# Latent attention's key rows copied in two groups of four, ScalarE copies of two output projections' banks, and a last stage that ends in token rows

## The reference, cut to what matters

```python
def sandwich(x, fn, pre_g, post_g, shift, scale, gate, res_w):
    hn = rmsnorm(x, pre_g) * (1 + scale[:, None, :]) + shift[:, None, :]
    y = rmsnorm(fn(hn), post_g)
    return x + res_w * gate[:, None, :] * y

def mla(h, w_in, q_norm, w_q_up, kv_norm, w_kv_up, w_o):
    ...
    k_rope = jnp.broadcast_to(rope(k_rope, pos), (B, S, MLA_HEADS, QK_ROPE))
    k = jnp.concatenate([kv[..., :QK_NOPE], k_rope.astype(kv.dtype)], axis=-1)
    ...
    return o.reshape(B, S, MLA_HEADS * V_HEAD) @ w_o

for i in range(2):
    # three sandwiches: ffn, mixer (latent attention for i = 0, dilated attention for i = 1), ffn
    x = sandwich(x, ffn_first, ...)
    x = sandwich(x, mixer, ...)
    x = sandwich(x, ffn_second, ...)
```

## Time and profile before

| | us |
|---|---|
| median of 3 runs | 4057.21 |
| lowest, highest | 4056.83, 4060.22 |
| the profiled execution's own time | 4056.78 |
| its span in the trace | 4055.0 |
| TensorE busy in the span | 3844.4 |
| VectorE busy | 2327.4 |
| ScalarE busy | 1291.5 |
| mean granted TensorE clock, share of full | 0.967 |

### The profile page before, as it was taken

The page is one execution under the profiler, slowest core; times in us unless marked ns, Lnnn a source line. Parts: engine busy times, 40 slices in busy tenths (PEclk is TensorE's granted clock), DMA queues, the critical chain, the costliest instruction groups (busy, mean ns, idle before and its releaser), DMA issues.

```text
span 4055.0 us, 48035 instructions
## 1 busy us (share of the span) xinstructions
PE 3844.4 (95%) x19230; PEld 3121.4 (77%) x19230; DVE 2327.4 (57%) x3024; ACT 1291.5 (32%) x1689; POOL 824.1 (20%) x580
## 2 busy tenths in 40 slices
PE   7998999999899999998899999999999999989997
PEld 6676888777688878886677888788777877767886
DVE  5876555587655555575566545543744554565333
ACT  4453232345323232224542222222233323322212
POOL 2100544210054436542222620000000000000000
PEclk9998999999899999998999999999999999999999
DMA  5111544311154435542223543233222112112331
GB/s 154 56 42 55 151 140 140 99 58 47 47 152 140 140 109 156 143 130 58 58 61 90 156 117 96 73 104 94 73 84 71 55 60 81 58 52 70 98 103 52
DMA packets 556442, 377.73 MB, mean 93 GB/s; under 512 B 30122, under 2 KB 553867, under 8 KB 556219
## 3 DMA queue, kind: packets, MB, share of 16 engines
q1 hardware_dynamic: 555642, 372.55, 31.3%
q10 hardware_dynamic: 576, 2.10, 0.1%
HBM read 372.44 MB, written 2.17 MB: 92 GB/s over the span
## 4 chain that ended last, share of the span: by engine, by line
PE 80%; DVE 15%; ACT 3%; issue 2%; DMA 0%; DVEq 0%; ACTq 0%; SPq 0%
PE bank L441 60%; PE bank L477 5%; PE bank L449 3%; DVE w_lo L419 2%; PE bank L822 2%; PE bank L807 2%; PE bank L2006 1%; PE bank L2031 1%; DVE conv_sum L1146 1%; PE bank L2052 1%; DVE hgrn_scores L1315 1%; PE bank L815 1%; ACT w_hi L410 1%; DVE norm_tmp L1531 1%; DVE std L849 1%
## 5 line engine op out<-in xcount | busy, mean ns | idle before, releaser
L441 PE MATMUL bank<-H_hi,w_hi 128*128 128x512 f32 x2384 | 996.5, 418 | 0.1
L441 PE MATMUL bank<-H_hi,w_lo 128*128 128x512 f32 x2384 | 933.2, 391 | 0.0
L441 PE MATMUL bank<-H_lo,w_hi 128*128 128x512 f32 x2384 | 931.8, 391 | 0.0
L419 DVE TENSOR_TENSOR w_lo<-w_raw,w_hi 128x2048 fp32r<-128x2048 f32 (+3 forms) x285 | 735.6, 2581 | 261.7 <-ACT w_hi L410 251.9
L410 ACT ACTIVATE w_hi<-w_raw 128x2048 fp32r<-128x2048 f32 (+3 forms) x285 | 529.2, 1857 | 300.4 <-DMA w_raw<-in_ffn_w_up 132.2
L441 PE MATMUL bank<-U_hi,w_hi 128*128 128x512 f32 x1408 | 558.4, 397 | 16.1 <-DVE U_lo L1195 10.3
L441 PE MATMUL bank<-U_hi,w_lo 128*128 128x512 f32 x1408 | 551.7, 392 | 0.0
L441 PE MATMUL bank<-U_lo,w_hi 128*128 128x512 f32 x1408 | 551.1, 391 | 0.0
L441 PEld LDWEIGHTS bank<-H_hi,w_hi 128*128 128x128 f32 x2384 | 449.0, 188 | 122.1 <-issue 39.2
L441 PEld LDWEIGHTS bank<-H_lo,w_hi 128*128 128x128 f32 x2384 | 449.6, 189 | 101.5 <-issue 21.0
L441 PEld LDWEIGHTS bank<-H_hi,w_lo 128*128 128x128 f32 x2384 | 448.1, 188 | 98.0 <-issue 0.3
(11 more groups left out here) (344 smaller groups left out, 4905.4 us busy)
## 6 DMA issues: line engine op xcount, KB each, us to landing
w_mod_raw<-in_w_mod SPq DMA_DIRECT2D x144, 512.0 KB, 6.4
w_raw<-in_ffn_w_gate SPq DMA_DIRECT2D x88, 512.0 KB, 4.0
w_raw<-in_ffn_w_up SPq DMA_DIRECT2D x88, 512.0 KB, 5.3
w_raw<-in_dil_w_in SPq DMA_DIRECT2D x36, 1024.0 KB, 5.1
w_raw<-in_w_mlp_in SPq DMA_DIRECT2D x32, 1024.0 KB, 5.5
w_raw<-in_w_mlp_out SPq DMA_DIRECT2D x32, 1024.0 KB, 5.2
w_raw<-in_ffn_w_down SPq DMA_DIRECT2D x32, 1024.0 KB, 5.1
w_raw<-in_w_in SPq DMA_DIRECT2D x16, 1024.0 KB, 5.2
```

The lines of the kernel that those rows point to most:

```text
L419: dve.eng.tensor_tensor(WL[u % SLOTS][:, 0:n], RAW[u % SLOTS][:, 0:n], WH[u % SLOTS][:, 0:n].bitcast(F32), ALU.subtract).then_inc(lo_done. ...
L441: mm = pe.eng.matmul(bank[0:m, :], w[:, k, c0:c0 + m], r[:, k, :], start=(k == 0 and i == 0), stop=(k == kt - 1 and i == 2))
```

## The change

It has three parts.

1. In latent attention ScalarE's eight copies of the rotated key rows become two groups of four. The first (slots of heads 0 to 3) stands in part 0 between the second and the third evacuation of `mla_kv`; the other (heads 4 to 7) in part 1 at point 9. TensorE's scores wait for four copies at their first head and for four more at the fifth.
2. In `mla_out` and `dil_out` ScalarE copies each bank to `Y` (`out_act`), and VectorE (`out_dve`) is left with products and sums; it waits for the bank to be freed.
3. The last stage turns while it multiplies. TensorE weaves in four transposes of `X` after the third inner tile of tile t, and four of `Y` times its gate (made by VectorE in `XY`) after the sixth inner tile of tile t+1; ScalarE copies both to token rows (`XROW`, `YROW`). When the sums are known, VectorE does one pass of 1024 for each block of 128 tokens, `XROW + YROW * rstd`, and SyncE's queue stores each block. The spread of factors, the sixteen passes over `X`, `sync_all`, the epilogue's transposes and its copies are gone.

The diff, cut to its core (the unchanged parts and the removed epilogue are left out):

```diff
+        def turn_x(pe, t):
+            pe.eng.wait_ge(x_rows.sem, t)
+            for b in range(NB):
+                mm = pe.eng.transpose(banks[6][:, b * P:(b + 1) * P], X[:, t, b * P:(b + 1) * P], EYE)
+            mm.then_inc(x_turned.sem, x_turned.add())
+        def turn_y(pe, t):
+            pe.eng.wait_ge(y_gated.sem, t + 1)
+            pe.eng.wait_ge(y_rows.sem, t)
+            ...
+        def last_down_pe(pe):
+            at_point = {}
+            for t in range(DT):
+                at_point[8 * t + 2] = (turn_x, t)
+                at_point[8 * t + 13] = (turn_y, t)
...
+            for u in lin[("ffn_down", 1, 1, 2)]:
+                pe_unit(pe, u, weave)
+            pe_running_sums(pe)
+            turn_y(pe, DT - 1)
...
+                    row_copy(act, x_turned, banks[6], XROW, x_rows, t)
+                    if t:
+                        row_copy(act, y_turned, banks[7], YROW, y_rows, t - 1)
+                    place, turn = acc_place[units[u]["tiles_at"] + j]
+                    act.eng.wait_ge(acc_free[place].sem, turn)
+                    ...
+                    act.eng.activation(SQ[t % 2][:], Y[:, t, :], ACT.Square)...
+            act_std(act, D, True)
+            row_copy(act, y_turned, banks[7], YROW, y_rows, DT - 1)
...
+                    ve.tensor_tensor(Y[:, t, :], Y[:, t, :], bank[:], ALU.add)...
+                    if t >= 2:
+                        dve.eng.wait_ge(y_turned.sem, t - 1)
+                    ve.tensor_scalar(XY[t % 2][:], Y[:, t, :], AFF[:, 1, 1, t:t + 1], None, ALU.mult)...
...
+            for b in range(NB):
+                ve.scalar_tensor_tensor(XROW[:, b, :], YROW[:, b, :], RSTD[:, b:b + 1], XROW[:, b, :], ALU.mult, ALU.add)...
+        def store_rows(sp):
+            for b in range(NB):
+                sp.eng.wait_ge(out_rows.sem, b + 1)
+                sp.eng.dma_start(io["out"][0, b * P:(b + 1) * P, :], XROW[:, b, :])...
...
+        def out_act(act, stage, dil=1):
+            ...
+                    bank, free = acc_take(act, u, j)
+                    act.eng.activation(in_order(Y[:, t, :], dil), dilated(bank[:], dil), ACT.Copy)...
+                    if t >= 2:
+                        act.eng.wait_ge(sq_summed.sem, sq_summed.next(act, 0 if t == 3 else 1))
+                    act.eng.activation(SQ[t % 2][:], Y[:, t, :], ACT.Square)...
+        def out_dve(dve, stage, two):
+            ...
+                    dve.eng.wait_ge(acc_free[place].sem, turn)
+                    x_product(dve, t, two)
+                    if 1 <= t < DT - 1:
+                        add_squares(dve, t, two)
+                        add_products(dve, t)
+            split_lo(dve, lin[stage][-1] + AHEAD)
...
-                    if i == 0:
-                        pe.eng.wait_ge(key_rows.sem, key_rows.next(pe, 8))
+                    if i < 24:
+                        pe.eng.wait_ge(key_rows.sem, key_rows.next(pe, 4))
...
+            def rope_rows(part):
+                if part == 0:
+                    act.eng.wait_ge(mla_rows.sem, mla_rows.next(act))
+                for h in range(4):
+                    ae.activation(MK[NOPE:QK, mla_slot(4 * part + h), :], MK0[NOPE:QK, :], ACT.Copy)...
...
+                    if (part, p) in ((0, 13), (1, 9)):
+                        rope_rows(part)
```

More of the change, by code:

```diff
@@ new lines, in build @@
+        x_turned, x_rows, y_gated, y_turned, y_rows, out_rows, out_stored = (line(n) for n in (
+            "x_rows_turned", "x_rows_ready", "y_gated_ready", "y_rows_turned", "y_rows_ready", "out_rows_ready", "out_stored"))
+        def turn_x(pe, t):
[7 more added lines that the diff above has]
+            for b in range(NB):
+                mm = pe.eng.transpose(banks[7][:, b * P:(b + 1) * P], XY[t % 2][:, b * P:(b + 1) * P], EYE)
+            mm.then_inc(y_turned.sem, y_turned.add())
@@ new lines, in last_down_pe, with weave @@
+        def last_down_pe(pe):
[3 more added lines that the diff above has]
+                at_point[8 * t + 13] = (turn_y, t)
+            points = iter(range(8 * DT))
+            def weave():
+                turn, t = at_point.get(next(points), (None, 0))
+                if turn:
+                    turn(pe, t)
+            for u in lin[("ffn_down", 1, 1, 2)]:
+                pe_unit(pe, u, weave)
+            pe_running_sums(pe)
+            turn_y(pe, DT - 1)
@@ new lines, in last_down_dve @@
+        def last_down_dve(dve):
+            stage, ve = ("ffn_down", 1, 1, 2), dve.eng
+            for u in lin[stage]:
+                if u != lin[stage][-1]:
+                    split_lo(dve, u + AHEAD)
+                for j in range(2):
+                    t = 2 * (u - lin[stage][0]) + j
+                    if t >= 2:
+                        add_squares(dve, t - 1)
+                    bank, free = acc_take(dve, u, j)
+                    ve.tensor_tensor(Y[:, t, :], Y[:, t, :], bank[:], ALU.add).then_inc(free.sem, free.add())
+                    dve.eng.wait_ge(free.sem, free.made)
+                    if t >= 2:
+                        dve.eng.wait_ge(y_turned.sem, t - 1)
+                    ve.tensor_scalar(XY[t % 2][:], Y[:, t, :], AFF[:, 1, 1, t:t + 1], None, ALU.mult).then_inc(y_gated.sem, y_gated.add())
+                    dve.eng.wait_ge(y_gated.sem, y_gated.made)
+            dve.eng.wait_ge(std_ready.sem, std_ready.next(dve))
+            ve.reciprocal(RSTD[:, 0:NB], STD[:, 0:NB]).then_inc(dve.step.sem, dve.step.add())
+            dve.eng.wait_ge(dve.step.sem, dve.step.made)
+            dve.eng.wait_ge(x_rows.sem, DT)
+            dve.eng.wait_ge(y_rows.sem, DT)
+            for b in range(NB):
+                ve.scalar_tensor_tensor(XROW[:, b, :], YROW[:, b, :], RSTD[:, b:b + 1], XROW[:, b, :], ALU.mult, ALU.add).then_inc(out_rows.sem, out_rows.add())
+                dve.eng.wait_ge(out_rows.sem, out_rows.made)
@@ L1571, in build @@
+        def store_rows(sp):
+            for b in range(NB):
+                sp.eng.wait_ge(out_rows.sem, b + 1)
+                sp.eng.dma_start(io["out"][0, b * P:(b + 1) * P, :], XROW[:, b, :]).then_inc(out_stored.sem, out_stored.add(16))
+            sp.eng.wait_ge(out_stored.sem, out_stored.made)
         SG = [at(f"silu_gate{i}", e_at + 2 * K * i, [P, L]) for i in range(2)]
@@ L1831, in mla_act @@
                             att_act_step(act, items, mla_bufs, kind, i)
-                if part == 0:
-                    act.eng.wait_ge(mla_rows.sem, mla_rows.next(act))
-                    for h in range(8):
-                        ae.activation(MK[NOPE:QK, h, :], MK0[NOPE:QK, :], ACT.Copy).then_inc(key_rows.sem, key_rows.add())
-                        act.eng.wait_ge(key_rows.sem, key_rows.made)
-            act_linear(act, ("mla_out",), running_squares(("mla_out",), y_tile), later=True, early=lin[("mla_out",)][:-1])
+            out_act(act, ("mla_out",))
         mla_rows = line("mla_key_rope_rows")
@@ L1890, in mla_dve @@
             sandwich_next(dve, 0, 1)
-            dve_linear(dve, ("mla_out",), to_y(("mla_out",), False, two=1), later=True, early=lin[("mla_out",)][:-1])
+            out_dve(dve, ("mla_out",), 1)
         CHUNKS = 3 * NB
@@ L2243, in dil_dve @@
             sandwich_next(dve, 1, 1)
-            dve_linear(dve, ("dil_out",), to_y(("dil_out",), False, dil=NB, two=0), later=True, early=lin[("dil_out",)][:-1])
+            out_dve(dve, ("dil_out",), 0)
         def second_pe(pe):
@@ L2493, in _ @@
                     dil_sp(sp, c)
+            store_rows(sp)
         @block.gpsimd
```

93 lines of the change are left out of this document (53 added, 40 removed).

## The result

| | before | changed |
|---|---|---|
| median, run side by side (4 runs each) | 4058.72 us | 4030.32 us |
| lowest to highest | 4056.83 to 4060.82 | 4029.13 to 4031.78 |
| span of the profiled execution | 4055.0 | 4028.2 |

The ratio is 0.993, with a 95% interval from 0.9913 to 0.9947, that is 22 to 35 us less. The forecast was 29.3 us less, at 4027.9; measured are 28.4 less, at 4030.32. Of the 2.4 us between forecast and median 1.5 lie in the kernel before, whose median was 1.5 us higher this time.

The account below looks back on a forecast made before the run. TensorE, busy 3844.4 of 4055.0 us, was taken as the bound, other engines costing time only where it waits. Gains of 3.1 + 6.7 + 8.1 + 11.4 = 29.3 us off 4057.2 gave 4027.9, range 4020 to 4037.

Parts of the forecast that it names:

- Key rows: Latent attention's first scores: start 3.4 us earlier, less 0.3 for the second four copies; 3.1 us gained, from 0.8 to 4.8.
- mla_out's border: Sums behind mla_out start earlier and run faster, less GpSimd's interference: 6.7 us gained, from 4.3 to 9.2.
- I take the middle, 4.4: Start of mla_out's border sums: 4.4 us earlier, between 3.7 (two copies beside GpSimd save nothing) and 5.1.
- The clock: mla_out's border: three to four of five groups of sums at the high clock, 3.0 us gained, from 2.0 to 4.1.
- GpSimd in the border: mla_out's border: GpSimd's next vector meets the first passes, a loss of 0.7 us, from 0 to 1.4.
- dil_out's border: Behind dil_out, GpSimd idle: seven copies save 5.1 us, the clock 3.0; 8.1 us gained, from 6.3 to 9.7.
- The end: Last stage and after: 6.6 us of woven transposes, then 12.4 us to the end instead of 30.4; 11.4 us gained.
- the woven group: Last stage: four transposes between matmuls cost 0.36 + 0.08 = 0.44 us a group, 6.6 us for 15 groups.
- Half of the borders' gain lost: Rival, both borders: ScalarE's and VectorE's waits on each other, or an earlier clock fall, leave some 8 of 15 us; chance 0.14.
- Woven transposes that wait: Rival, last stage: each of 15 groups waits some 1.5 us for ScalarE's previous copy, 22 us, time 4050; chance 0.04.
- The clock falling in the last stage: Rival: the stream with transposes is granted 1.2 GHz, 43.5 us more, time 4071, slower; chance 0.02.
- The key rows' gain is eaten: Rival, latent attention: the second four copies land on the path, 1 us or nothing gained, time 4030; no chance of its own.

Follow-up runs that it names:

- keys_only: The kernel before with only the key rows' copies in two groups of four: 4057.42 us beside 4058.92, ratio 0.9995.
- out_only: The kernel before with only ScalarE's bank copies in mla_out and dil_out: 4043.52 us, ratio 0.9958.
- before_mods: The kernel before with only GpSimd's modulation steps at latent attention's first scores and mla_out moved later: 4044.92 us beside 4061.23, ratio 0.9959.
- heads: The changed kernel with each head's first scores waiting for their own query row instead of all four: 4034.32 us.
- scores_free: The changed kernel with GpSimd's modulation steps moved later from mla_out, its border and the first scores, including the one beside the query rows: 4029.23 us.

## Why the prediction was right, and where a term was off

The forecast was 29.3 us and the medians give 28.4, but 0.9 us of difference says little, since the interval is 14 us wide. The stretches say more. What can be laid to the change is 3.5 + 4.9 + 0.8 + 7.7 + 10.9 = 27.8 us (the 0.8 is dil_out's fifth tile). So the mechanisms were right, and that the total came so near is in part luck, since errors of both signs stand in it.

**Key rows, 3.1 forecast, 3.5 and 3.0 measured.** Right in each step but the clock's: the releaser is the query rows, the start is 3.40 us earlier (forecast 3.4), and across the second four copies in part 1 the lead shrinks by 0.4 us (forecast 0.3; VectorE's maxima come 3.38 us earlier ahead of them and 2.98 behind in keys_only). The sum took the low clock for the scores. It was high here and low right behind, which took the difference back; in keys_only it was low, as assumed.

**mla_out's border, 6.7 forecast, 4.9 measured.** Three terms were too good by some. The start: 4.4 taken between 3.7 and 5.1, measured 3.6 (5.42 - 1.79). Beside GpSimd a tile's four passes and the copy took 6.02 us before, and the four passes alone take 6.03 now, so the two copies saved nothing, and five copies of 0.725 are 3.6. The step that failed is "I take the middle, 4.4": the trace spoke for the lower end. The Trainium skill, in SBUF — State Buffer, section Who interferes with whom, says that a VectorE instruction with at most one SBUF input, outside the two-port modes, does not contend with GpSimd. The trace agrees, with 0.69 us for the copies, and by the prediction's own reading of that rule the lower end, 3.7, was the one to take. The clock: 3.0 forecast, 2.4 measured, with three fast groups and not four. GpSimd in the border: 0.7 forecast, 1.05 measured, 1.0 of it in one addition of four columns that took 1.16 us instead of 0.16.

**dil_out's border, 8.1 forecast, 7.7 measured, and 0.8 ahead of it.** VectorE's work up to the last addition of squares is 5.4 us shorter, by the seven copies (5.1) and an idle row of 0.38 us. The early start of TensorE's fifth tile, put at 0.5 and left out of the sum, takes 0.8 us of this into the stretch ahead, so the sums start 4.7 us earlier against TensorE's last record, and the clock gives 3.0. The other 1.6 us of the stretch ahead lie in code that the change left alone. The two borders in between give 1.25 (28.01 against 26.76) and lose 0.68 (28.88 against 29.56), as the clock falls later or earlier among their matmuls; the rest, 1.0 us, stays open.

**The end, 11.4 forecast, 10.9 measured.** The chain behind the last matmul is 12.4 us as forecast, with four passes of 1.285 (forecast 1.30). The term that was too small is the woven group. A woven group costs 7.24 / 15 = 0.48 us, not 0.44: the row that I priced it by shows the matmul behind the transposes, and the next few matmuls are slower by some hundredths too (0.23 to 0.24 apart instead of 0.227).

**The rivals.** Half of the borders' gain lost: no, 12.6 of 14.8 us came, and in out_only neither VectorE nor TensorE waits for a bank copy's turn. Woven transposes that wait: no, no row copy holds TensorE. The clock falling in the last stage: no, it was granted 1.00 over 50.75 us. The Trainium skill, in TensorE: Matmul & The Clock Gate, Part 4: PE-mode transpose, says that transposes don't count as busy time of TensorE in the same way as matmuls; with some 7 us of them in 50 that showed nowhere.

*The key rows' gain is eaten:* no, 3.0 us stayed in keys_only.

What the prediction didn't see is how much larger GpSimd's share was than the part that it priced: before_mods gains 16.3 us in its medians (13.7 by stretches) with no copy moved, about as much as ScalarE's copies in both stages together (15.4, and 15.0 by stretches).

## What to carry to other kernels

Before work is moved off an engine that is late, look at what makes its operations longer than they are elsewhere: here four passes beside GpSimd took 6.0 us instead of 3.0, and taking a copy out from between them saved nothing. Compare traces by stretches cut at the same instructions; where no fall of the clock lies in one, it agrees to hundredths, while times of whole runs spread over 10 us. When an idle row names a releaser, work out what is next behind it first: the wait of 1.6 us ahead of the scores could be removed for a gain of 0.4 us (heads), or with its cause for 4.0 by mla_out's last record (scores_free). Before an engine's steps are moved to later places, look for who needs the last of them: one unit too late cost 13 us.

## What the runs showed of the hardware

- VectorE's additions of 32x512 took 5.8 us for four beside GpSimd and 2.84 us without. A one-input copy from a bank kept its 0.69 us beside GpSimd.
- An operation on 128x4 numbers of `x_squares`, 0.16 us long elsewhere, took 1.12 to 1.85 us seven times in five of the twelve traces. Each time an addition of GpSimd had started 0.06 to 0.17 us before it, and the small operation ended 0.02 to 0.03 us after that addition. In the changed kernel it was the one of 1.16 us.
- VectorE's split of 128x1152 took 2.85 us beside GpSimd's additions and 1.36 us without.
- The same code, untouched, took 1895.1 to 1902.7 us from the start to the rotation of the queries in the twelve traces. Added up from the granted clock in windows of 20 us, which is an estimate, some 124 us of it went at 1.2 GHz in the shortest and some 143 us in the longest. Stretches without a fall of the clock, as the 305.8 us ahead of the last stage, agree within 0.07 us.
- ScalarE copies a bank of 128x512 in 0.60 us and VectorE in 0.69.
